# A chunked gated delta rule whose triangular inverse is computed in another way, in a two-block transformer kernel

## What is computed

```python
a_mat = einsum("bclhd,bcshd->bclsh", k, k) * beta[:, :, :, None] * masked_exp(diff, strict)
lhs = moveaxis(a_mat, -1, 2) + eye(CHUNK)                 # unit lower triangular
rhs = concatenate([v * beta[..., None], k * (beta * exp(g))[..., None]], -1)
sol = triangular_solve(lhs, moveaxis(rhs, 3, 2), left_side=True, lower=True, unit_diagonal=True)
u, w = sol[..., :dv], sol[..., dv:]
...
    v_new = u_c - einsum("bhlk,bhkv->bhlv", w_c, s)
    o = einsum("bhlk,bhkv->bhlv", qg_c, s) + einsum("bhls,bhsv->bhlv", qk_c, v_new)
    s = s * dec_c[..., None, None] + einsum("bhlk,bhlv->bhkv", kd_c, v_new)
```

## Time and profile before

| | |
|---|---|
| median of 3 runs | 1867.92 us (1863.32 to 1871.38) |
| the profiled execution | 1869.31 us |
| its span in the profile | 1867.6 us |
| PE busy | 1708.2 us, 91% of the span |
| DVE busy | 684.6 us, 37% |
| ACT busy | 435.7 us, 23% |
| POOL busy | 213.2 us, 11% |
| DMA | 372.69 MB, 200 GB/s over the span |

### The profile page before, as it was taken

How to read it: one execution, slowest core, us unless ns; L and a number is a source line. 1 busy time by engine, 2 the same in 40 slices (tenths; PEclk the granted TensorE clock), 3 DMA queues, 4 the chain that set the end, 5 groups by cost and what they waited for, 6 DMA issues and landing times.

```text
span 1867.6 us, 25449 instructions
## 1 busy us (share of the span) xinstructions
PE 1708.2 (91%) x10656; PEld 1209.9 (65%) x10656; DVE 684.6 (37%) x1404; ACT 435.7 (23%) x889; POOL 213.2 (11%) x190
## 2 busy tenths in 40 slices
PE   7999999999888879999999899899989989699996
PEld 3558555456666547767766588666978874488842
DVE  2107113335434353323233377665355450400003
ACT  1010454013111123323332231322333430000000
POOL 2000000020000012221212100011342320100000
PEclk9999999998988889999999899999999999799998
DMA  7444335723999888979989434224121222244340
GB/s 242 163 148 143 128 125 190 251 103 135 372 394 350 326 317 343 416 318 365 415 340 393 171 137 148 90 91 176 62 91 46 91 91 90 90 138 178 123 155 38
DMA packets 124295, 372.69 MB, mean 200 GB/s; under 512 B 10523, under 2 KB 26517, under 8 KB 107413
## 3 DMA queue, kind: packets, MB, share of 16 engines
q1 hardware_dynamic: 118245, 361.12, 51.6%
q0 software_dynamic: 1568, 8.39, 1.2%
q10 hardware_dynamic: 4368, 1.54, 0.4%
HBM read 369.98 MB, written 1.05 MB: 199 GB/s over the span
## 4 chain that ended last, share of the span: by engine, by line
PE 77%; DMA 13%; DVE 7%; ACT 1%; issue 1%; SPq 0%; DVEq 0%; ACTq 0%
PE psum L1976 49%; PE psum L571 10%; DMA ring<-in_w_down 4%; PE psum L1775 4%; DMA ring<-in_w_up 4%; DMA ring<-in_w_in 4%; PE psum L1970 3%; PE psum L1816 2%; PE psum L1759 2%; PE psum L1797 1%; PE psum L2093 1%; PE psum L768 1%; PE psum L2123 1%; PE psum L557 1%; DVE area L1180 1%
## 5 line engine op out<-in xcount | busy, mean ns | idle before, releaser
L1976 PE MATMUL psum<-area,ring 128*128 128x256 f32 x1984 | 457.7, 391 | 15.1 <-DMA ring<-in_w_in 14.1
L1976 PE MATMUL psum<-ring,area 128*128 128x512 f32 (+1 forms) x1040 | 452.5, 595 | 8.6 <-DMA ring<-in_w_proj_mem 2.4
L1976 PEld LDWEIGHTS psum<-area,ring 128*128 128x128 f32 x1984 | 386.1, 197 | 75.2 <-DMA ring<-in_w_in 18.1
L1976 PEld LDWEIGHTS psum<-ring,area 128*128 128x128 f32 x1040 | 198.9, 193 | 252.7 <-issue 251.7
L571 PEld LDWEIGHTS psum<-area 128*128 128x128 f32 x2304 | 269.7, 194 | 34.7 <-issue 19.1
L571 PE MATMUL psum<-area 128*128 128x128 f32 x2304 | 281.0, 280 | 10.6 <-DVE area L1180 10.4
L949 ACT ACTIVATE area<-psum 128x512 f32<-128x512 f32 x236 | 138.7, 597 | 243.7 <-PE psum L571 127.8
L2249 ACT ACTIVATE area<-psum 128x512 f32<-128x512 f32 x116 | 66.4, 599 | 460.9 <-PE psum L1976 362.2
L1970 PE MATMUL psum<-const,area 128*128 128x128 f32 x736 | 120.6, 294 | 52.0 <-DVE area L1490 14.8
L1970 PEld LDWEIGHTS psum<-const,area 128*128 128x128 f32 x736 | 90.5, 149 | 97.4 <-issue 23.0
L1775 PE MATMUL psum<-ring,area 128*32 128x256 f32 x2048 | 124.8, 388 | 12.5 <-DMA ring<-in_w_up 12.3
(11 more groups left out here) (304 smaller groups left out, 1346.5 us busy)
## 6 DMA issues: line engine op xcount, KB each, us to landing
ring<-in_w_gate SPq DMA_DIRECT2D x64, 1024.0 KB, 9.6
ring<-in_w_up SPq DMA_DIRECT2D x64, 1024.0 KB, 11.5
ring<-in_w_down SPq DMA_DIRECT2D x64, 1024.0 KB, 11.3
ring<-in_w_in SPq DMA_DIRECT2D x29, 2048.0 KB, 8.4
ring<-in_w_ada SPq DMA_DIRECT2D x12, 2048.0 KB, 8.1
ring<-in_w_in SPq DMA_DIRECT2D x13, 1024.0 KB, 7.5
ring<-in_w_out SPq DMA_DIRECT2D x6, 2048.0 KB, 8.5
ring<-in_w_ffn_gate SPq DMA_DIRECT2D x5, 2048.0 KB, 7.8
```

What stands on the lines that cost most here:

```text
L1976: last = nc.tensor.matmul(dst, lhs(k), rhs(k), start=first and k == 0, stop=final and k == count - 1)
```

## The change

The delta rule's step is rewritten, and its two halves are no longer in one phase.

- **Blocks.** The powers and their products (AT, P2, X2, X4, X8) go. Instead DVE cuts the diagonal 16x16 blocks out of A, folds them to 128x16 per head (`rows`), and spreads them (phase compact). PE multiplies with the block mask to give every row of a block all of the block's entries (two products of 128x512, phase rep), ACT copies them, and DVE runs a recurrence of 15 steps with two instructions each, every one waiting for the one before (phase solve). Its result, the transposed block inverse, is spread to 128x128 by four instructions.
- **Levels.** They work on X^T. Per level and half: one transpose (X), one product with the level's part of A (V), one product (Y), a subtraction on DVE. The product T of before is gone, ACT still copies two tiles.
- **w.** With a state, K S is computed and scaled by ACT, DVE subtracts it from beta v (`r_ready`), and one product applies X. The products w and the second half of v go.
- **Running sums** over rows (`gR`, and `ssd_rows` in the scan of the latent side) are now transposes of a broadcast column of `cum`.
- **Streams.** Each half has a list of 13 phases (rows, gram, compact, rep, solve, X0, Y0, X1, Y1, X2, Y2, v, S). `staggered` runs the first half six phases ahead of the second, and then takes one phase of each in turn. The costs in `context_phases` are new, so the mixed stage's order changes too; pieces of the latent side hang on other phases.

```diff
+STAGGER = 6
+def staggered(first, second):
+    for _ in range(STAGGER):
+        yield "0 " + next(first)
+    while True:
+        phases = [("1 ", next(second, None)), ("0 ", next(first, None))]
...
-    gdn = [("rows", 3.1), ("gram", 1.9), ("AT", 1.2), ("P2", 3.8), ("X2", 5.7), ("X4", 3.8), ("X8", 1.9), ("XT0", 1.2),
+    costs = {"rows": 1.2, "gram": 1.0, "compact": 0.5, "rep": 1.8, "solve": 0.5, "X0": 1.6, "Y0": 1.0, "X1": 1.6, "Y1": 1.0,
+             "X2": 2.1, "Y2": 1.0, "v": 1.0, "S": 1.0}
...
+            pe.wait_ge(s["spread_ready"], 2 * m + h + 1)
+            for i in range(2):
+                pair = slice(2 * i, 2 * i + 2)
+                nc.tensor.matmul(open_tile(("gRep", m, h, i)), blk16, b["spread"][:, pair, :, :].rearrange("p h i j -> p (h i j)"),
+                                 start=True, stop=True).then_inc(filled, 1)
...
+                transposes(("gX", m, h, lev), [b["XT"][:, i, :] for i in range(4)])
+                pe.wait_ge(s[f"levels_{h}"], 3 * m + lev + 1)
+                four(("gV", m, h, lev), lambda i: b["AL"][:, i, :], lambda i: b["XT"][:, i, :])
...
-                        last = nc.tensor.matmul(dst[:, j * P:(j + 1) * P],
-                                                log_a[1][:, c - 2, d, 4 * q + j:4 * q + j + 1].to_broadcast([P, P]),
-                                                (upto, since)[d], start=True, stop=True)
+                        last = nc.tensor.transpose(dst[:, j * P:(j + 1) * P],
+                                                   cum[1][:, d, c - 2, 4 * q + j:4 * q + j + 1].to_broadcast([P, P]), ident)
...
+            link(v.tensor_tensor(block, b["A"], blk16.unsqueeze(1).to_broadcast([P, 4, P]), ALU.mult))
+            link(v.tensor_reduce(rows, block.rearrange("p h (g j) -> p h j g", j=16), AX.X, ALU.add))
+            for i in range(4):
+                ins = v.tensor_tensor(b["spread"][:, i, :, :], rows[:, i, :].unsqueeze(1).to_broadcast([P, 16, 16]),
+                                      unit_16.unsqueeze(2).to_broadcast([P, 16, 16]), ALU.mult)
...
+            for j in (range(15), range(15, 0, -1))[d]:
+                left = (slice(j + 1, 16), slice(0, j))[d]
+                n = left.stop - left.start
+                link(v.tensor_tensor(tmp[:, :, 0:n], rep[:, :, left, j], Y[:, :, j:j + 1].to_broadcast([P, 4, n]), ALU.mult))
+                link(v.tensor_tensor(Y[:, :, left], Y[:, :, left], tmp[:, :, 0:n], ALU.subtract))
```

553 lines of the change are left out of this document (231 added, 322 removed).

## The result

| | before | after |
|---|---|---|
| median | 1865.6 us (1862.9 to 1871.4) | 1915.6 us (1909.0 to 1922.9) |
| ratio, 95% interval | | 1.027 (1.022 to 1.031) |
| the profiled execution | 1869.3 us | 1922.9 us |

The change makes the kernel 2.7% slower. The prediction had 1838 us, and 1884 us as the upper end of its range.

A forecast was written before the change was run, and what follows sets the result against it. PE was taken to set the pace, the mixed stage's queue close behind, with DVE becoming fullest in the latent delta rule. Gains of 20 (mixed), 7 (scan) and 4 us (latent) took 1869.3 to 1838; range 1797 to 1884.

The forecast's parts named there:

- three terms: Forecast gains by stage: 20 us in the mixed stage, 7 in the latent side's scan, 4 in the latent delta rule.
- charted period of 54.5 us: Latent delta rule: one step laid out engine by engine gave 53 us, taken as 54.5 for the lower clock.
- 15.8 us per expert: Mixed stage, second part: expert period falls from 16.8 us, 14.6 by PE's work plus 1.2 of waits; gain 18 us.
- lead-in: Latent delta rule: time up to the first half's first X0 on PE, taken as 21 us.
- up to 3 us more per period: Latent delta rule: extra cost at the lower clock of PE tiles that lead to the next DVE work.
- The cover by the other half: Delta rule steps: a solve of one half, 8.0 us on DVE, runs beside PE's levels of the other.
- Single waits don't stop the queue; the mean counts: Mixed stage: the ring of six slots covers a PE wait of up to 15 us, so only mean waits matter.
- lower bound of 3 us: Scan of the latent side: least gain from turning 64 products into transposes; 7 us forecast, upper bound 8.
- The solve in DVE's list is the new bound: Rival, chance 0.13: 16 solves of 8 us delay other DVE work; mixed +10, latent +20, scan -7, 1892 us.
- a period of 61 with the clock low through both rests: Latent delta rule, worst bound: solves at 9.1 us, stage 253 us, a loss of 15.
- three worst bounds: Worst case per stage: mixed stage 20 us lost, latent delta rule 15 lost, scan only 3 gained.
- three signs of being wrong: Chained pair over 0.6 us, latent periods below 48 or above 60, queue under 0.9 in the mixed stage's second part.

The follow-up runs named there:

- e2: The changed kernel with 14 of the 15 recurrence steps left out of each solve (a probe, computes something else); 1829.0 us, 0.977 of before.
- e3: The changed kernel with unused products added on PE ahead of each wait for a solve; 1907.9 us, 1.020 of before.
- e4: The changed kernel with POOL's delta rule masks and products cut to 8 elements per partition (a probe, computes something else); 1893.5 us, 1.012 of before.
- e5: The changed kernel with STAGGER 1 instead of 6, both halves going through the phases together; 1908.6 us, 1.021 of before.
- e7: The changed kernel with the second half's recurrence and spreading on POOL instead of DVE; 1944.2 us, 1.039 of before.
- e8: The changed kernel with the mixed schedule's costs raised, solve 0.5 to 6.0 and compact 0.5 to 2.0; 1898.5 us, 1.015 of before.
- e13: e8 with the short solve of e2 (a probe, computes something else); 1817.4 us, 0.973 of before.
- e9: The changed kernel with STAGGER 1, one solve for both halves, real work moved into PE's and DVE's rests, joint phases' costs raised; 1884.5 us, 1.009 of before.

## Why the prediction was wrong

The prediction summed 1869.3 - 20 - 7 - 4 = 1838. In profiled time the three terms came out at +21, +1 and +33. Two steps failed, and both fed the sum. In the latent part it was the charted period of 54.5 us, which had 1.5 us for the lower clock and nothing for POOL. In the mixed stage it was the 15.8 us per expert, which had nothing for the lower clock and let waits for solves replace waits for weights. What each experiment gives back overlaps with the others (61, 14 and 21 us of 33 in the latent part), so these prices do not add up to the loss. Point by point:

- **Prices of single operations.** Right for the chain (7.5 us with 6.7 forecast, 0.5 of it because its first instruction was held up, and its spreading 0.9 with 1.1) and for most of DVE's work: 180 us forecast, 190 measured. (The forecast multiplied by 41.1 where its own step had 41.8; that is 3 us.) DVE did not become the fullest engine: PE was busy 192 us. Two terms were too small: compact, whose reduction takes 1.01 us and not 0.69, and whose spreading takes up to 3.18 instead of 1.43 beside POOL. POOL as a user of what DVE needs was in no term of the sum.
- **The charted period.** This is the step that failed in the latent part: 54.5 us taken, 64.3 measured. Three periods are 29 of the 37 us between -4 and +33; the lead-in was 22 us (21 forecast), and the last step with what follows took the other 7. The chart had the waits before the levels nearly right, 4 and 7 us (5.1 and 7.0 measured, at 1432.64 and 1465.07). What stood between them was laid out at full clock. PE was charted with 37 us of work per step and was busy 48. The clock, with "up to 3 us more per period" and 1.5 taken, is the term that was mis-sized. PE was busy for 72 us at the lower level, where the same work takes about twice the time (8 records 1.92 us and 1.06), so the clock cost PE up to 36 us, 9 a period. In e2 PE was busy for 29 us at that level, and 20 us less in all for the same records. With half of that time taken off, both kernels have 156 to 157 us of PE. How much of the 9 lies on the chain is told only by e3, which gives back 8 to 14 us net, 2 to 3.5 a period. The omitted term is POOL, 21 us in e4, 5 a period, in part through the same chain.
- **The cover by the other half.** The chart took it that solve and copies of one half lie beside the other's levels. e2 and e5 deny it: a solve taken away comes off in full, and the stagger taken away costs nothing. e7 shows that it is the length of the chain (compact, rep, ACT, solve, levels) that counts, and not the list of DVE.
- **The mixed stage.** "Single waits don't stop the queue; the mean counts" is the sentence that failed. PE's waits for solves and compact were 28.7 and 10.1 us, 31 in the forecast. But they did not take the place of waits for weights: from 700 us on those rose from 14.0 to 21.5 us (up and down weights), where 0.5 us per expert, 9 in all, was to go. And the work taken off PE, 56 us by its prices, lowered its busy time by 27 only: 58 us of it lay at the lower clock, 49 more than before, and half of that, 25 us, is nearly all that is missing. The forecast had no clock term here. Where waits for compact, solve and key norms stood in a row the queue fell to a share of 0.34, and 23 us of lead were lost in four issues. e8 shows that 18 us of the stage are a matter of order. The solve's length is 25 to 31 us (e2, e13). From 765 us on an expert took (1027.66 - 765.22) / 15 = 17.5 us, with 15.8 forecast; the kernel before took (1007.98 - 752.49) / 15 = 17.0 for the same ones.
- **The scan.** The lower bound of 3 us failed. PE was spared 3.7 us of busy time in the stage, the wait for DVE's mask took their place, and 0.6 us of the 7 arrived in the changed kernel. The prediction called PE "hardly idle there"; the wait of 7.7 us that was already there pointed to DVE.
- **The rivals.** "The solve in DVE's list is the new bound" had the right sign in each stage, and both conditions were met or nearly so (a period of 64.3, over 58; waits of PE (28.7 + 10.1) / 18 = 2.2 us per expert, just under the 2.3 named). Its price was too low: +10 in the mixed stage and +20 in the latent part, measured +21 and +33, and its gain in the scan did not come. It was given a chance of 0.13. Its condition in the latent part was met and its mechanism is the one that came, but as the chain's length and not as DVE's list (e7). The Trainium skill's section named beside it (TensorE: Matmul & The Clock Gate, "HAM oscillation") describes idle stretches that return and a clock that falls each time; the trace agrees, with 0.82 where 0.97 was.
- **The range.** Its upper bound for the latent part, a period of 61 with the clock low through both rests, priced the rests but not all the products behind them, which run at the low clock too. The range was also narrower than its parts: its upper end, 1884, lay below the rival's own 1892 and below the sum of the three worst bounds (1869.3 + 20 + 15 - 3 = 1901). Two of the three signs of being wrong came, periods above 60 and a queue under 0.9 (0.83); a chained pair stayed at 0.4 to 0.5 us.

By the fixed term of about 150 cycles that the Trainium skill gives (VectorE: DVE Perf Modes, "The TRN2 errata") a chain would have been an estimated 5.7 us. Here instructions of 4 elements in a chain start 0.20 us apart and those of 56 to 60 elements 0.25 to 0.28, so the trace decides for 7.0, and 7.5 with the first one held up.

## What to carry to other kernels

Work taken off a nearly full engine is worth nothing where a serial chain across engines takes its place: chart the chain at the price of the lower clock behind each wait, and count every engine's part. Where a chain is unavoidable, put real work of the waiting engine's own list ahead of its wait (e9, 18 us of the stage, 13 by the medians). A schedule made from the chain's length and not from the engine's busy time gave 18 us in e8 and nothing in e9, so look whether the order that comes out puts work beside the chain on every engine. Two streams in fixed lists hide each other's chains only if that is shown, and undoing the stagger is a cheap test.

## What the runs showed of the hardware

A DVE instruction with both inputs in SBUF was held up by one on POOL until that one was over. The first of the chain above started at 1424.17 and took 0.75 us, the next took 0.22, and this ran on POOL until 1424.83:

```profile
1423.56 1.27 POOL L1495 TENSOR_TENSOR area<-area,const 128x512 f32<-128x512 f32 x1 [4.60 <-PE psum L608]
```

Four spreads took 3.18 us beside POOL and 1.43 alone. A chained instruction on POOL took 0.63 us where its neighbours took 0.28; it ended at 1430.80, behind DVE's at 1430.68, so it acts both ways. The Trainium skill says that DVE and GpSimd take turns on one pair of SBUF ports, for a whole instruction, also when the DVE instruction has two SBUF inputs and the GpSimd one reads SBUF (SBUF — State Buffer, "SBUF: two separate sides"). These rows agree, and the prediction should have used it.

A chained small instruction on POOL starts 0.28 us after the one before it at 4 elements and 0.40 at 60; on DVE it is 0.20 at 4 and 0.25 to 0.28 at 56 to 60.
